# FFN down as a block product of seven products, with the third weight sum made by GpSimd

## The reference

```python
def conv_ffn(h, lp, rows, cols):
    gate, val = jnp.split(h @ lp["ffn_w_up"], 2, axis=-1)
    gate = dwconv_grid(gate, lp["ffn_conv_w"], lp["ffn_conv_b"], rows, cols)
    return (jax.nn.silu(gate) * val) @ lp["ffn_w_down"]
...
        x = x + g2 * conv_ffn(hx, lp, rows, GRID_W)
...
    return rms_norm(x, final_g)
```

## Time and profile before

| | us |
|---|---|
| median of three runs | 2270.85 |
| lowest, highest run | 2262.39, 2271.01 |
| span of the profiled execution | 2265.7 |
| TensorE matmuls, VectorE busy in it | 2050.2, 1500.4 |
| ScalarE, GpSimd busy in it | 892.1, 773.6 |
| FFN-down stage, first to last matmul | 1324.4 to 1579.8 |

### The profile page before, as it was taken

The page is one execution under the profiler, slowest core; times in us unless marked ns, Lnnn a source line. Parts: engine busy times, 40 slices in busy tenths (PEclk is TensorE's granted clock), DMA queues, the critical chain, the costliest instruction groups (busy, mean ns, idle before and its releaser), DMA issues. The chain is left out here.

```text
span 2265.7 us, 37012 instructions
## 1 busy us (share of the span) xinstructions
PE 2050.2 (90%) x15072; PEld 1594.0 (70%) x15072; DVE 1500.4 (66%) x2052; ACT 892.1 (39%) x1445; POOL 773.6 (34%) x460
## 2 busy tenths in 40 slices
PE   4989999837878898999999979999899999999898
PEld 1767677636767676788877768887677776776566
DVE  5777767679774548788988870454746676546644
ACT  5453443414434637333333331443434354333320
POOL 1144433300030145877777724533321111111111
PEclk7999999958899999999999999999999999999899
DMA  7535444597655422122221274523211111102512
GB/s 308 182 122 174 151 141 130 154 264 197 167 177 143 159 75 75 56 84 84 84 76 73 84 272 139 177 73 122 85 56 56 66 38 47 66 19 84 195 47 84
DMA packets 181335, 271.16 MB, mean 120 GB/s; under 512 B 74280, under 2 KB 122024, under 8 KB 176816
## 3 DMA queue, kind: packets, MB, share of 16 engines
q1 hardware_dynamic: 164816, 250.57, 33.9%
q10 hardware_dynamic: 16352, 18.22, 2.7%
HBM read 200.53 MB, written 68.23 MB: 119 GB/s over the span
## 5 line engine op out<-in xcount | busy, mean ns | idle before, releaser
L105 PE MATMUL b_ps<-h_hi,b_wpool 128*128 128x512 f32 (+1 forms) x896 | 277.4, 387 | 10.8 <-POOL b_wpool L744 10.8
L2995 PE MATMUL g_ps<-g_h_hi,w 128*128 128x512 f32 x784 | 260.0, 403 | 6.0 <-ACT g_q L3192 5.9
L3313 POOL TENSOR_TENSOR w<-raw_down,w 128x1024 fp32r<-128x1024 f32 x38 | 94.5, 2488 | 464.6 <-ACT w L3168 464.6
L2262 DVE SCALAR_TENSOR_TENSOR e_vars<-grid,vec,e_vars 128x1024 f32<-128x1024 f32 x168 | 216.0, 1285 | 7.4 <-ACT e_vars L2009 4.2
L105 PEld LDWEIGHTS b_ps<-h_hi,b_wpool 128*128 128x128 f32 x896 | 167.8, 192 | 56.3 <-POOL b_wpool L744 14.4
L2995 PEld LDWEIGHTS g_ps<-g_h_hi,w 128*128 128x128 f32 x784 | 149.3, 190 | 40.8 <-ACT g_q L3192 6.9
L105 PE MATMUL b_ps<-h_lo,b_wpool 128*128 128x512 f32 (+1 forms) x448 | 170.6, 381 | 0.0
L2995 PE MATMUL g_ps<-g_h_lo,w 128*128 128x512 f32 x392 | 156.1, 398 | 0.0
L2674 POOL TENSOR_TENSOR g_down_lo<-raw_down,g_down_hi 128x1408 fp32r<-128x1408 f32 x26 | 86.7, 3339 | 142.5 <-ACT g_down_hi L2574 142.5
L2513 PE MATMUL g_pb<-g_z_hi,g_down_hi 128*128 128x512 f32 x286 | 114.8, 401 | 14.7 <-DVE g_down_lo L2751 9.8
L744 POOL TENSOR_TENSOR b_wpool<-raw_in,b_wpool 128x1024 fp32r<-128x1024 f32 x26 | 67.9, 2611 | 173.2 <-ACT b_wpool L530 173.2
(11 more groups left out here) (524 smaller groups left out, 5284.4 us busy)
## 6 DMA issues: line engine op xcount, KB each, us to landing
e_raw_up<-w_ffn SPq DMA_DIRECT2D x22, 1024.0 KB, 4.9
raw_down<-w_down SPq DMA_DIRECT2D x32, 704.0 KB, 4.2
c_op<-ops SPq DMA_DIRECT2D x40, 512.0 KB, 5.0
raw_down<-w SPq DMA_DIRECT2D x38, 512.0 KB, 3.7
raw_in<-w SPq DMA_DIRECT2D x26, 512.0 KB, 4.2
mod_stage<-ada_rows ACTq DMA_DIRECT2D x24, 512.0 KB, 3.7
zs<-e_z SPq DMA_DIRECT2D x21, 512.0 KB, 2.6
ops<-b_xin SPq DMA_DIRECT2D x20, 512.0 KB, 4.7
```

Source lines behind the costliest of these rows:

```text
L105: last = nc.tensor.matmul(out, w[:, k, :], x[:, k, cols], start=(k == 0 and n == 0), stop=(k == nk - 1 and n == 2))
L2262: STT(out=acc, in0=view, scalar=wt, in1=acc, op0=ALU.mult, op1=ALU.add).then_inc(sem("conv"), 1)
L2995: mm = nc.tensor.matmul(out_bank, ww[w % 2][:, k], xx[g][:, k], start=(k == 0 and a == 0), stop=(k == KD - 1 and a == 2))
L3313: nc.gpsimd.tensor_tensor(w_lo[w % 2], raw[:, w % 2], w_hi[w % 2].bitcast(F32), ALU.subtract).then_inc(sem("lo"), 1)
```

## The change

The product W x Z is cut in 2 x 2 blocks: W in output features (tiles 0-3, 4-7) and hidden width (two times 11 tiles), Z in hidden width and positions. Call the weight blocks A11, A12 (output tiles 0-3, first and second half of the width), A21, A22 (tiles 4-7), and the result blocks c11, c12 (tiles 0-3, positions 0-511 and 512-1023), c21, c22. The eight block products become seven:

- P1 = A11 with z(0,0) and P2 = A12 with z(1,0), the first number being the half of the width and the second the half of the positions
- P7 = S3 T3, P6 = S2 T2, P4 = A22 T4, P5 = S1 T1, P3 = S4 z(1,1)
- S1 = A21 + A22, S3 = A11 - A21, S2 = S1 - A11, S4 = A12 - S2
- T3 = z(1,1) - z(0,1), T2 = T3 + z(0,0), T4 = z(1,0) - T2, T1 = z(0,1) - z(0,0)

Each product has four units, so there are 28 units of 33 matmuls. The order is P1, P2, then P7 and P6 in turn for each of four rows of tiles p, then P4, P5, P3. All 16 weight sums (four of each S) are made by GpSimd with 128x1408 elements, each ahead of the split into high and low part; that includes the third, S2, which is `sum_s2`. S1 and S2 are stored in memory (`sums_down`) and loaded again for P5 and S4. The operand sums T (`t_sum`, 24 instructions) are made by VectorE. Every operand is split anew: 36 low parts by VectorE and six, those of P2, by GpSimd. P6 is needed in three result blocks together with P1, so ScalarE keeps P1 in an SBUF buffer `u2`, VectorE adds P6, and the three additions read `u2`. There are 44 additions to x, before 16. z pieces are loaded 54 times, before 22 times; two halves of the positions are finished later than before: c11 after P2, c21 after P4, c22 after P5, c12 after P3. The normalising of half 0 starts when unit 22, the third of P5, is done.

The core of the diff (a line of dots stands for lines left out; the transfers' queue is shown for one pair):

```diff
+    P1, P2, P7, P6, P4, P5, P3 = ORDER = range(7)
+    UNITS = ([(P1, p) for p in range(FOUR)] + [(P2, p) for p in range(FOUR)] + [(x, p) for p in range(FOUR) for x in (P7, P6)]
+             + [(x, p) for x in (P4, P5, P3) for p in range(FOUR)])
...
+    SHARED = UNITS[FOUR:20] + [(P3, 0), (P3, 1)]
+    bank_of = lambda x, p: mem["rot"][SHARED.index((x, p)) % 2] if (x, p) in SHARED else mem["kept"][p]
+    u2 = mem["u2"]
...
+    KS = [list(range(KD)), list(range(FOUR, KD)) + list(range(FOUR))]
...
+    def store_s2(sp, p):
+        sp.wait_ge(sem("w_s2"), p + 1)
+        sp.dma_start(d["sums_down"][1, p], w_place(("A11", p))).then_inc(sem("s2_stored"), 16)
...
+        after_low(sp, 6)
+        load_tile(sp, ("A11", 0), 0, 0)
+        load_z(sp, Z_T2)
+        load_z(sp, Z_T2 + 1)
+        store_s1(sp, 0)
+        load_x(sp, 1, 2)
+        after_low(sp, 7)
+        load_tile(sp, ("A21", 1), FOUR + 1, 0)
+        for q in range(Z_T2 + 2, Z_T4):
+            load_z(sp, q)
+        store_s2(sp, 0)
+        sp.wait_ge(sem("s1_stored"), 16)
+        load_tile(sp, ("A22", 1), FOUR + 1, 1)
+        after_low(sp, 8)
+        load_tile(sp, ("A11", 1), 1, 0)
...
+        if (o, p) in SHARED:
+            at = SHARED.index((o, p))
+            if at < 2:
+                pe.wait_ge(sem("silu_late"), 1)
+            else:
+                pe.wait_ge(sem("added"), last_read(*SHARED[at - 2]))
+        elif o == P5:
+            pe.wait_ge(sem("u2"), p + 1)
+        elif o == P3:
+            pe.wait_ge(sem("added"), last_read(P5, p))
...
+        elif o == P7:
+            act.wait_ge(sem("w_sum"), 2 * p + 2)
+        elif o == P6:
+            act.wait_ge(sem("w_s2"), p + 1)
+        elif o == P3:
+            act.wait_ge(sem("w_sum"), 2 * FOUR + p + 1)
...
+    def squares(act, g, i):
+        k = KS[g][i]
+        act.wait_ge(sem("added"), final_of(g, k))
+        if i == 0 and g:
+            act.wait_ge(sem("h_lo"), KD)
+        elif i >= 2:
+            act.wait_ge(sem("folded"), g * (KD - 1) + i - 1)
...
+    def keep_p1(act, p):
+        act.wait_ge(sem("unit"), made(P1, p))
+        if p:
+            act.wait_ge(sem("added"), last_read(P6, p - 1))
+        nc.scalar.activation(u2, bank_of(P1, p), ACT.Copy).then_inc(sem("p1_kept"), 1)
...
+        split_w(act, 5)
+        for r in range(3):
+            split_x(act, P7, r)
+        split_w(act, 6)
+        for r in range(3, NP):
+            split_x(act, P7, r)
+        split_w(act, 7)
+        split_w(act, 8)
+        keep_p1(act, 0)
+        split_w(act, 9)
+        for r in range(NP):
+            split_x(act, P6, r)
+        for p in range(1, FOUR):
+            split_w(act, 8 + 2 * p)
+            squares(act, 0, p - 1)
+            split_w(act, 9 + 2 * p)
+            keep_p1(act, p)
...
+        split_w(act, 23)
         for a in range(2):
             root(act, 0, a)
+        after_low(act, 17)
+        split_w(act, 24)
         for k in range(4):
             high(act, 0, k)
+        split_w(act, 25)
         for k in range(4, KD):
             high(act, 0, k)
+        for i in range(3):
+            squares(act, 1, i)
+        split_w(act, 26)
+        for i in range(3, 5):
+            squares(act, 1, i)
+        split_w(act, 27)
...
+    def sum_s1(pool, p):
+        nc.gpsimd.tensor_tensor(w_place(("A22", p)), w_place(("A21", p)), w_place(("A22", p)), ALU.add).then_inc(sem("w_sum"), 1)
...
+    def sum_s3(pool, p):
+        nc.gpsimd.tensor_tensor(w_place(("A21", p)), w_place(("A11", p)), w_place(("A21", p)), ALU.subtract).then_inc(sem("w_sum"), 1)
...
+    def sum_s4(pool, p):
+        nc.gpsimd.tensor_tensor(w_place(("A12", p)), w_place(("A12", p)), w_place(("S2", p)), ALU.subtract).then_inc(sem("w_sum"), 1)
...
     def gpsimd(pool):
-        for n in range(NU):
-            if n != 1:
-                pool.wait_ge(sem("w_hi"), n + 1)
-                nc.gpsimd.tensor_tensor(w_lo[w_slot(n)], raw[:, n % 2], w_hi[w_slot(n)].bitcast(F32),
-                                        ALU.subtract).then_inc(sem(f"w_lo{n % 2}"), 1)
+        lo = lambda n: low_w(pool, nc.gpsimd, n)
+        lo(0)
+        lo(2)
+        for r in range(3):
+            low_x(pool, nc.gpsimd, P2, r)
+        lo(3)
+        low_x(pool, nc.gpsimd, P2, 3)
+        lo(4)
+        for r in range(4, NP):
+            low_x(pool, nc.gpsimd, P2, r)
+        lo(5)
+        lo(6)
+        sum_s1(pool, 0)
+        sum_s3(pool, 0)
+        lo(7)
+        sum_s2(pool, 0)
+        lo(8)
+        for p in range(1, FOUR):
+            lo(7 + 2 * p)
+            sum_s1(pool, p)
+            sum_s3(pool, p)
+            lo(8 + 2 * p)
+            sum_s2(pool, p)
+        for n in range(15, 24):
+            lo(n)
+        sum_s4(pool, 0)
+        lo(24)
+        sum_s4(pool, 1)
+        lo(25)
+        sum_s4(pool, 2)
+        sum_s4(pool, 3)
+        lo(26)
+        lo(27)
...
+    def sum_s2(pool, p):
+        pool.wait_ge(sem("w_sum"), 2 * p + 2)
+        nc.gpsimd.tensor_tensor(w_place(("A11", p)), w_place(("A22", p)), w_place(("A11", p)), ALU.subtract).then_inc(sem("w_s2"), 1)
...
+    def t_sum(dve, o, r):
+        if o == P7:
+            a, b = Z_T3 + 2 * r, Z_T3 + 2 * r + 1
+            z_there(dve, a)
+            z_there(dve, b)
+            dve.wait_ge(sem("unit"), 3)
+            TT(turned_of(r), z_part(a), z_part(b), ALU.subtract).then_inc(sem("t_sum"), 1)
...
+    def sum_u2(dve, p):
+        dve.wait_ge(sem("unit"), made(P6, p))
+        dve.wait_ge(sem("p1_kept"), p + 1)
+        TT(u2, u2, bank_of(P6, p), ALU.add).then_inc(sem("u2"), 1)
...
+        for r in range(NP):
+            low_of(P6, r)
+        def add_p6(p):
+            sum_u2(dve, p)
+            for c in ("c21", "c22", "c12"):
+                add(dve, c, P6, p)
+
+        for p in range(FOUR):
+            add(dve, "c21", P7, p)
+            add(dve, "c22", P7, p)
+            if p < FOUR - 1:
+                t_sum(dve, P4, 2 * p)
+                t_sum(dve, P4, 2 * p + 1)
+                add_p6(p)
+                if p:
+                    fold(dve, 0, p)
...
+        add(dve, "c22", P5, 1)
+        add(dve, "c12", P5, 1)
         dve.wait_ge(sem("gain"), 1)
         mean(dve, 0)
         norm_out(dve, 0)
+        for p in range(2, FOUR):
+            add(dve, "c22", P5, p)
+            add(dve, "c12", P5, p)
+        add(dve, "c12", P3, 0)
+        for i in range(1, 4):
+            fold(dve, 1, i)
+        add(dve, "c12", P3, 1)
+        fold(dve, 1, 4)
+        fold(dve, 1, 5)
+        add(dve, "c12", P3, 2)
+        fold(dve, 1, 6)
```

585 lines of the change are left out of this document (379 added, 206 removed).

## The result

The changed kernel takes 2330.4 us (median of four runs, 2319.4 to 2336.3) against 2268.0 us for the kernel before (2262.4 to 2271.0, four runs on the same chip): 1.028 times as long, with a 95% interval of 1.0245 to 1.031. The forecast was 2293 us with a range up to 2312. The direction was right, the size was not: 62 us slower instead of 22.

A forecast was written before the change was run, and what follows sets the result against it. FFN-down was taken as matmul-bound; with fewer matmuls, GpSimd and VectorE turn-taking can't all hide. 211.4 + 2.4 + 1.3 + 7 + 24 + 29 + 2.3 = 277.4 us against 255.4, 22 more: 2293 us, range 2267 to 2312.

The forecast's parts named there:

- P4 and the first three units of P5: ... Nothing lost.: Units of P4 and first three of P5: one GpSimd low part per unit, covered by its idle time; 0 us lost.
- Slow restarts, 2.3 us.: Unit 26 and one or two others restart with matmuls at half clock after waits; 2.3 us on the path.
- the clock drops at every wait: Rival: each of eight waiting units restarts slowly at 1.6 to 2.4 us; 15 us more, 2308 us, chance 0.14.
- the forecast's own case: Whole kernel: waits outweigh the matmuls removed, 22 us slower, 2293 us; chance 0.58.
- P1 and P2, 7 us, bounds 2 and 12.: First eight units: unit 6 late by 2.2, unit 7 by 3.5, unit 8 by 1; 7 us, bounds 2 and 12.
- P7 and P6, 24 us.: Next eight units: GpSimd's five ops per pair and turns with VectorE make pairs 22 to 25 us; 24 lost, bounds 12, 32.
- The end, 29 us.: After unit 22: unit 26 waits behind half 0's normalising, VectorE's fold, ScalarE's split, GpSimd's low part; 29 late, bounds 13, 35.
- "... whatever the order, it can't all hide": Whole stage: GpSimd and VectorE work with SBUF inputs takes turns, 257 us against 215 us of matmuls.
- The other rivals: Whole kernel: blocking counts less, 2259 us, chance 0.11; about half, waits of 40 us, 2271 us, chance 0.17.
- the signs named for the forecast: GpSimd busy over 155 us, VectorE subtractions 3-4, low-part waits 20 and more over units 9-15, over 15 before unit 26.
- a sign of being wrong altogether: In the stage: GpSimd's 1408-column sums differ from 3.2 us, or VectorE's ops from u2 don't wait.

The follow-up runs named there:

- e10: On top of e4: sums of P5's operand go to the turned rows, freeing both places at once, and weight 19's load is issued earlier; 2313.4 us, ratio 1.021.
- e4: Changed kernel with only queue order changed in P4, P5, P3: weight splits and additions ahead of operand pieces that wait for transfers; 2330.7 us, ratio 1.027.
- e3: Changed kernel with all 16 weight sums computed on 1 of 11 tiles only, all transfers kept; 2292.7 us, ratio 1.013.
- e9: Changed kernel reordered in P2, P4/P5/P3 and the end, with s1, s3 and s2 of all four pairs on VectorE; 2320.4 us, ratio 1.024.
- e1: Changed kernel with the four s2 sums moved back from GpSimd to VectorE; 2324.1 us, ratio 1.027.
- e2: Changed kernel with the four s2 sums left on GpSimd but computed on 1 of 11 tiles only; 2322.6 us, ratio 1.025.
- e7: Changed kernel with only the order at the end changed: additions and splits of weights 24 to 26 moved ahead of normalising work; 2323.5 us, ratio 1.023.
- e11: On top of e7: low part 26 ahead of the fourth s4, weight 27 split after two squares, folds between x3 products; 2323.2 us, ratio 1.026.
- e5: Changed kernel with each operand-piece transfer from P7's operand on moving 8 of 128 partitions; 2313.7 us, ratio 1.022.

## Why the prediction was wrong

The stage was forecast at 277.4 us and took 319.9 in the profiled execution, 42.5 more. TensorE is not busy in 17.6, 15.8, 22.6 and 21.8 us of the four parts, 78 us in all, where the forecast had waits of 7, 24, 0 and 29, together 60; the rest of the difference is slow matmuls. By the prediction's own steps:

**"P4 and the first three units of P5: ... Nothing lost."** This step failed, by 29.8 us. It looked at GpSimd's one low part per unit, for which there was room (22.55 us busy in 82.68), and not at P5's operand. P5 is the one product besides P7 whose every piece is a difference of two transfers, with two pairs of places. For P7 the prediction did name this ("a place is free only after the sum before it, and a transfer takes 3.8 to 6.2 us") and then charged it 7 us; for P5 it did not ask. The numbers were there: six pieces, two ahead, four turns of a transfer of some 5 us, sum 1.2, low part 1.2: about 30 us, as long as P4's four units, and the first sum comes 9 us into P4 (1507.34 against 1497.97). Weight splits, additions and weight loads stand behind these pieces in three queues, so units wait long before the operand itself is needed. e10, with e4's order, freed places and weight 19's load moved ahead, leaves 3.7 us.

**Slow restarts, 2.3 us.** Also failed, by some 20 us. TensorE is busy 242.0 us for 932 matmuls (264 + 264 + 233 + 171), 0.260 each, against 249.03 for 1061, 0.235, in the earlier trace rows: 23 us more for the same matmuls. After the wait of 15.76 us the timeline shows them 0.43 us apart from 1630.78 to about 1636, at half the clock of 2.4 GHz, and the granted clock is 0.82 to 0.90 in every part; in e3's P7/P6 and e10's P4, where hardly any waits are left, it is 1.00. These 23 us lie inside the losses of the four parts (about 3, 9, 5 and 6 by their rows). So half of what the forecast missed is here. The rest is waits: 23 and 11 us more in P4/P5 and P1/P2, less 8 and 7 in P7/P6 and the end. The rival "the clock drops at every wait", given 15 us and a chance of 0.14, happened, beside the forecast's own case and not instead of it: all seven waits of 4.8 us and more are followed by matmuls 0.43 us apart, of the eight between 1.0 and 3.9 us two at once (2.05, 2.09), two after four or five matmuls (2.86, 3.94) and four not at all. The Trainium skill, TensorE: Matmul & The Clock Gate, "HAM oscillation — how this bites in real kernels", says that a kernel with a wait in each turn starts each turn cold; the trace agrees for the waits of 4.8 us and more.

**P1 and P2, 7 us, bounds 2 and 12.** Mis-sized, beyond its bound: 19.7, and 19.0 to 19.8 in the other executions of this code. The place was right and the mechanism in part: unit 6, which was given 2.2 us, waits 12.45. Its weight's low part is ready at 1384.1, 6.5 us after unit 5's end (1377.7), by the path of the forecast; the last 6 us are for VectorE's addition, which frees the bank and which the forecast did not have. ScalarE's split of its weight stands behind the third piece of P7's operand, and VectorE's addition behind a sum of pieces and a low part, held back by GpSimd's low part 6 and its first sum:

```profile
1378.59 1.06 ACT L2738 ACTIVATE g_z_hi<-g_turned_rows 128x1024 fp32r<-128x1024 f32 x1 [4.71 <-DVE g_turned_rows L2943]
1379.55 1.36 ACT L2759 ACTIVATE g_down_hi<-raw_down 128x1408 fp32r<-128x1408 f32 x1
...
1380.99 3.15 POOL L2763 TENSOR_TENSOR g_down_lo<-raw_down,g_down_hi 128x1408 fp32r<-128x1408 f32 x1 [12.98 <-ACT g_down_hi L2759]
1384.09 4.14 POOL L2884 TENSOR_TENSOR g_beside_rows<-g_down_extra,g_beside_rows 128x1408 f32<-128x1408 f32 x1
...
1381.98 3.23 DVE L2943 TENSOR_TENSOR g_turned_rows<-g_v,ahead_of_sq 128x1024 f32<-128x1024 f32 x1 [2.29 <-issue]
...
1385.80 3.51 DVE L2743 TENSOR_TENSOR g_z_hi<-g_turned_rows,g_z_hi 128x1024 fp32r<-128x1024 f32 x1
1389.23 0.74 DVE L2972 SCALAR_TENSOR_TENSOR x<-g_pb,mod,x 128x512 f32<-128x512 f32 x1
...
1390.12 1.19 PE L2676 MATMUL g_pb<-g_z_lo,g_down_hi 128*128 128x512 f32 x2 [12.45 <-DVE x L2972]
```

**P7 and P6, 24 us.** 26.1, inside the bounds. But 9 of it are slow matmuls, and TensorE is idle for only 15.8 us, so the nearness of the number is luck. The pairs take 28.2, 18.2, 22.1 and 18.0 us where 22 to 25 were expected. GpSimd's chain of five ops and turns with VectorE is the cause (e3, e9). The share of the moved sums is about 5 us over P1 to P6 (e1, e2).

**The end, 29 us.** 29.1, with its steps each within 4 us. Here too 6 us are slow matmuls and the idle time is 21.8, so again the exact hit is luck. e7 and e11 show that it was the order of the queues that put the normalising ahead of unit 26, as the prediction said, and that better order gains 15 us inside the stage, of which 10 come back behind it.

**"... whatever the order, it can't all hide"** (257 us of turn-taking work under 215 of matmuls) holds as far as the runs go: thirteen of them change order or places, and the shortest stage is 260.8 us, with GpSimd relieved of every sum. No run tests the count itself: with 16 sums at 1.6 us on VectorE instead of 3.2 on GpSimd it is some 231 us there. The range was too narrow: 2312 is the sum with the upper bounds 12, 32 and 35. P1/P2 alone passed its bound by 8 us, and a part called free had no upper bound.

The other rivals fell: the time is neither near 2259 nor 2271. Of the signs named for the forecast, four came: GpSimd busy 166.4 us in the stage, VectorE's subtractions at 3 to 4.3 us beside it, no pair of 17 us or less, the wait ahead of unit 26. Two did not. Low parts of weights are waited for by 7.9 us between units 9 and 15, not 20 and more; the largest wait there, 5.81 us ahead of unit 9, is for VectorE's low parts of P6's operand. And s1, s3 and s2 take 3.2 to 4.3 us, not near 3.2, which was named as a sign of being wrong altogether; they lengthen beside VectorE's ops, as the low parts do.

## What to carry to other kernels

When a change cuts matmuls by adding sums of operands, draw for each operand the loop that makes it (transfer, sum, split, low part, place free, next transfer), multiply it by the pieces that don't fit the places, and compare it with the matmuls that run meanwhile, and look at what stands behind these pieces in every queue, the one that issues transfers included; a stretch in which no engine is over 75% busy can be the one that loses most. Give a sum its output where it frees both inputs' places at once. Count slow restarts for every wait of several us, and give an upper bound also to the parts that you call free.

## What the runs showed of the hardware

A transfer of a sixteenth of the bytes took 2.2 us from issue to the sum behind it (1500.71 to 1502.90 in e5), where a whole piece of 512 KB took 4.7 (1512.48 to 1517.13): nearly half of the time was still there. The Trainium skill, DMA: Bandwidth & Descriptors, "Rules for kernel authors", advises to issue early and wait late so that a fixed cost is overlapped; e10 issues pieces and a weight's load earlier, and lost 20 us less in its part than e4.

Short waits can be cheap for the clock: in e10's P4 the granted clock stayed 1.00 with some 2 us of short waits left in the part, while the waits of 9 and 16 us in the changed kernel were each followed by matmuls 0.43 us apart. But its wait of 2.09 us ahead of unit 25 was followed by seven such matmuls.

Under turn-taking GpSimd's ops also lengthen, not only VectorE's: 3.95 to 4.17 us beside VectorE's ops against 3.2 alone. In P7/P6 GpSimd is busy 61.35 us in 17 ops, 3.6 each; five per pair are then 18 us where the sum said 16.
